# A fused attention and expert layer: the last expert's rows placed by a zero-one product, and the two partial sums of a tile added on Pool

## The reference

```python
x = layer_norm(DN_ALPHA * x + fox_mixer(x, ...), ln1_g[0], ln1_b[0])
y = moe(x, ...)
x = layer_norm(DN_ALPHA * x + y, ln2_g[0], ln2_b[0])

def moe(...):                 # the routed part
    # each token goes to 8 of 64 experts, with weights w
    def body(acc, blk):
        rows, rw, e = blk
        xb = x_pad[rows]
        h = jax.nn.silu(xb @ w_gate[e]) * (xb @ w_up[e])
        yb = (h @ w_down[e]) * rw[:, None]
        return acc.at[rows].add(yb), None
    shared = (jax.nn.silu(xf @ ws_gate) * (xf @ ws_up)) @ ws_down
    return acc[:T] + shared

def layer_norm(x, g, b):
    mu = jnp.mean(x, -1, keepdims=True)
    var = jnp.mean(jnp.square(x - mu), -1, keepdims=True)
    return (x - mu) * lax.rsqrt(var + LN_EPS) * g + b
```

## Time and profile before

| | |
|---|---|
| median of 3 runs | 1689.19 us (1687.73 to 1690.91) |
| profiled execution, its own time | 1685.87 us |
| its span, first to last instruction | 1684.2 us |
| busy share PE, DVE, ACT, POOL | 93%, 70%, 61%, 31% |
| mean granted clock of PE | 0.964 of full speed |

### The profile page before, as it was taken

How to read it: one execution, slowest core, us unless ns; L and a number is a source line. 1 busy time by engine, 2 the same in 40 slices (tenths; PEclk the granted TensorE clock), 3 DMA queues, 4 the chain that set the end, 5 groups by cost and what they waited for, 6 DMA issues and landing times.

```text
span 1684.2 us, 31748 instructions
## 1 busy us (share of the span) xinstructions
PE 1565.4 (93%) x8182; PEld 1306.1 (78%) x8183; DVE 1181.8 (70%) x2034; ACT 1027.7 (61%) x1700; POOL 514.2 (31%) x486
## 2 busy tenths in 40 slices
PE   6999999999998998998999999999999999999960
PEld 6897888888887776786878878888788878788840
DVE  3215777777778777746777867777677778778827
ACT  3215666666667544336667867667676777678823
POOL 0000000000000145423455445455455554465320
PEclk9999999999999998998999999999999999999975
DMA  7223221222224425569899999989998999999957
GB/s 239 88 79 98 65 70 46 69 57 62 69 50 138 177 107 177 190 212 345 238 304 312 324 360 334 306 251 285 314 318 256 306 362 314 359 355 351 365 125 294
DMA packets 161508, 369.25 MB, mean 219 GB/s; under 512 B 53040, under 2 KB 73520, under 8 KB 161456
## 3 DMA queue, kind: packets, MB, share of 16 engines
q1 hardware_dynamic: 136272, 284.21, 48.4%
q0 software_dynamic: 25184, 84.39, 19.7%
HBM read 294.39 MB, written 65.77 MB: 214 GB/s over the span
## 4 chain that ended last, share of the span: by engine, by line
PE 66%; DMA 11%; DVE 9%; issue 6%; ACT 3%; POOL 1%; POOLq 1%; ACTq 1%; another core or an unknown queue 0%; SPq 0%; DVEq 0%
DMA sums_scratch<-ys,sidx 7%; PE bank L993 5%; PE bank L996 5%; PE bank L999 5%; PE out_ps L884 4%; PE q_ps L88 4%; PE q_ps L90 4%; PE q_ps L89 4%; PE out_ps L1051 3%; PE k_ps L863 3%; PE out_ps L1052 3%; PE k_ps L1020 3%; PE q_ps L983 3%; PE k_ps L1021 3%; PE k_ps L1028 2%
## 5 line engine op out<-in xcount | busy, mean ns | idle before, releaser
L1836 DVE TENSOR_TENSOR gu_lo<-raw_gu,gu_hi 128x1024 fp32r<-128x1024 f32 x260 | 306.4, 1220 | 25.2 <-ACT gu_hi L1330 24.1
L1330 ACT CAST gu_hi<-raw_gu 128x1024 fp32r<-128x1024 f32 x260 | 253.3, 1050 | 2.3 <-DMA raw_gu<-in_moe_w_gate_dram 1.2
L993 PE MATMUL bank<-gu_hi,xb_hi 128*128 128x512 f32 x576 | 233.9, 406 | 6.2 <-DVE gu_lo L1836 3.1
L996 PE MATMUL bank<-gu_lo,xb_hi 128*128 128x512 f32 x576 | 227.9, 396 | 0.0
L664 POOL DMA_INDIRECT sums_scratch<-ys,sidx x64 | 122.6, 1916 | 155.3 <-DMA sums_scratch<-ys,sidx 112.5
L1836 DVE TENSOR_TENSOR dn_lo<-raw_dn,dn_hi 128x1024 fp32r<-128x1024 f32 x130 | 152.3, 1209 | 3.7 <-ACT dn_hi L1330 3.7
L999 PE MATMUL bank<-gu_hi,xb_lo 128*128 128x512 f32 x576 | 142.5, 389 | 0.0
L643 POOL DMA_INDIRECT x_rows<-rows_scratch,gidx x64 | 83.6, 1306 | 173.8 <-DVE wcol L1852 141.2
L993 PEld LDWEIGHTS bank<-gu_hi,xb_hi 128*128 128x128 f32 x576 | 110.6, 192 | 29.7 <-issue 7.5
L1330 ACT CAST dn_hi<-raw_dn 128x1024 fp32r<-128x1024 f32 x130 | 130.0, 1051 | 3.2 <-DMA raw_dn<-in_moe_w_down_dram 3.2
L599 POOL IOTA e<- 128x64 f32 x1 | 0.2, 190 | 427.6 <-DVE xs L1632 427.6
(11 more groups left out here) (276 smaller groups left out, 3934.6 us busy)
## 6 DMA issues: line engine op xcount, KB each, us to landing
raw_gu<-in_moe_w_gate_dram SPq DMA_DIRECT2D x128, 512.0 KB
raw_gu<-in_moe_w_up_dram SPq DMA_DIRECT2D x128, 512.0 KB
raw_dn<-in_moe_w_down_dram SPq DMA_DIRECT2D x128, 512.0 KB
wqk<-in_fox_w_in_dram SPq DMA_DIRECT2D x66, 128.0 KB, 2.5
v_scratch<-v_out SPq DMA_DIRECT2D x32, 256.0 KB, 2.8
va<-v_scratch SPq DMA_DIRECT2D x16, 512.0 KB, 4.7
xs<-in_x_dram SPq DMA_DIRECT2D x8, 512.0 KB, 7.8
wv<-in_fox_w_in_dram SPq DMA_DIRECT2D x4, 1024.0 KB, 6.1
```

What stands on the lines that cost most here:

```text
L993: i = pe.matmul(o3, xb_hi[s][:, c], g_hi[:, :, c], start=c == 0, stop=False, skip_group_check=True)
L996: pe.matmul(o3, xb_hi[s][:, c], g_lo[:, :, c], start=False, stop=False, skip_group_check=True)
L1330: a.copy(hi, raw).then_inc(S[done], 1)
L1836: dve.tensor_tensor(lo, raw, hi, ALU.subtract).then_inc(S[lo_ok], 1)
```

## The change

The first rows and the last further block of expert 63 are no longer added in memory.

- ACT and DVE write the scaled rows of expert 63 as a high and a low part, `y_hi` and `y_lo` (128 x 1024), and the last further block as `yx_hi`, `yx_lo` (64 partitions: its two stacked halves).
- POOL writes `tokens` (an iota of 0 to 1023 on every partition); DVE compares it with the token of each row and gets a zero-one matrix `place_of` (128 rows by 1024 tokens), and `x_place` for the further rows. The tokens of the rows come from `tab` (`tok_f`, `tok_x`).
- PE multiplies: for each tile of 128 tokens, `place_of` with `y_hi` and `y_lo`, `x_place` with `yx_hi` and `yx_lo`, 8 matmuls of 128 x 512 into `q_ps` or `k_ps` in turns (`put_in_place`). The result is what expert 63 adds to each token of the tile.
- On PE the first rows of expert 63 now go in front of the end of its further block: `turn_h` before `gate_up_further`, `down` before `turn_h_further`.
- POOL no longer issues the two adds of expert 63. It raises `summed` before `add_first` of 62, and after that adds the two sums of each tile (`fin0 <- fin0 + fin1`, 128 x 1024, eight of them, semaphore `f_pair`).
- SP loads `sums[1]` of tiles 0 and 1 on `summed`, then waits for `sent[0]` and `sent[1]`, which now end with expert 62, then loads the rest.
- DVE's sum of a tile takes PE's PSUM tile and POOL's sum. g2 is copied once by ACT into `out_ps`, and DVE reads it there; the output tile is written over `fin1` instead of a buffer of its own.

```diff
@@ SP
             sp.wait_ge(S["g_lo_ok"], G_PIECES * (E + 1))
-            sp.wait_ge(S["set_free"], 1)
             sp.wait_ge(S["summed"], 1)
-            load_sums(1, 0)
+            for t in range(2):
+                load_sums(1, t)
             for i in range(2):
-                sp.wait_ge(sent[i], 8 * E + SENT_0[i])
-            for t in range(TT):
+                sp.wait_ge(sent[i], 8 * E + SENT_0[i] - 16 * i)
+            for t in range(2):
                 load_sums(0, t)
-                if t + 1 < TT:
-                    load_sums(1, t + 1)
+            for t in range(2, TT):
+                load_sums(1, t)
+                load_sums(0, t)
@@ POOL, in expert(63), ahead of add_first of 62
+                if ends:
+                    pool.wait_ge(S["d_lo_ok"], D_PIECES * E)
+                    g.iota(tokens[:], pattern=[[1, T]], base=0, channel_multiplier=0, allow_small_or_imprecise_dtypes=True).then_inc(S["f_pair"], 1)
...
+                        pool.sem_inc(S["summed"], 1)
                     add_first(1 - par, e - 1)
@@ POOL, the end
-            with pool.If(nx > 0):
-                add_further(E - 1, nx - 1, xi + nx - 1)
-            add_first(1, E - 1)
-            pool.wait_ge(sent[2], 16 * (xi + nx) + SENT_0[2])
-            stand(pool)
-            pool.sem_inc(S["summed"], 1)
+            for t in range(TT):
+                pool.wait_ge(tile_in[t], 16 * 3)
+                g.tensor_tensor(fin0[:, t], fin0[:, t], fin1[:, t], ALU.add).then_inc(S["f_pair"], 1)
@@ PE
+            def put_in_place(further_too):
+                for t in range(TT):
+                    to = slice(t * P, (t + 1) * P)
+                    if t == 0:
+                        pe.wait_ge(S["place_step"], 2)
+                    if t >= 2:
+                        pe.wait_ge(S["f_mean"], 2 * (t - 2) + 1)
+                    for r in HALVES:
+                        o = (q_ps, k_ps)[t % 2][:, r]
...
+                        pe.matmul(o, place_of[:, to], y_hi[:, r], start=True, stop=False, skip_group_check=True)
...
+                        i = pe.matmul(o, place_of[:, to], y_lo[:, r], start=False, stop=not further_too, skip_group_check=True)
...
+                            pe.matmul(o, x_place[:, to], yx_hi[:, r], start=False, stop=False, skip_group_check=True)
+                            i = pe.matmul(o, x_place[:, to], yx_lo[:, r], start=False, stop=True, skip_group_check=True)
@@ ACT
+                        last_y_hi(m, e)
+                        act.wait_ge(S["x_downed"], after)
+                        a.copy(yx_hi[:, 0:D], out_ps[0:2 * XR, :]).then_inc(S["y_hi_ok"], 1)
...
+                    a.copy(out_ps[:], g2[:]).then_inc(S["y_hi_ok"], 1)
@@ DVE
+            dve.tensor_scalar(place_of[:, 0:T], tokens[:], tok_f[:, 0:1], None, ALU.is_equal).then_inc(S["place_step"], 1)
...
+                dve.tensor_scalar(x_place[:], tokens[0:2 * XR], tok_x[:, 0:1], None, ALU.is_equal).then_inc(S["place_step"], 1)
...
-                    dve.tensor_tensor_reduce(out=fin0[:, t], in0=fin0[:, t], in1=fin1(t), scale=1.0, scalar=0.0, op0=ALU.add,
+                    dve.tensor_tensor_reduce(out=fin0[:, t], in0=(q_ps, k_ps)[i][:], in1=fin0[:, t], scale=1.0, scalar=0.0, op0=ALU.add,
...
-                    dve.scalar_tensor_tensor(out=fin2[:, t], in0=fin0[:, t], scalar=fnm[i][:, 0:1], in1=g2[:], op0=ALU.add,
+                    dve.scalar_tensor_tensor(out=fin1[:, t], in0=fin0[:, t], scalar=fnm[i][:, 0:1], in1=out_ps[:], op0=ALU.add,
```

More of the change, by code:

```diff
@@ L254, in build @@
             tab = sb("tab", [P, TAB], I32, c=m)
+            tok_f = sb("tok_f", [P, 1], c=m)
+            tok_x = sb("tok_x", [2 * XR, 1], c=m)
         with ExitStack() as f:
             fin0 = sb("fin0", [P, TT, D], c=f)
-            fin2 = sb("fin2", [P, TT, D], c=f)
+            y_hi = sb("y_hi", [P, D], F32R, c=f)
+            y_lo = sb("y_lo", [P, D], F32R, c=f)
+            tokens = sb("tokens", [P, T], c=f)
+            x_place = sb("x_place", [2 * XR, T], F32R, c=f)
+            place_of = sb("place_of", [P, T + E], F32R, c=f)
+            yx_hi = sb("yx_hi", [2 * XR, D + E], F32R, c=f)
+            yx_lo = sb("yx_lo", [2 * XR, D + E], F32R, c=f)
             g2 = sb("g2", [P, D], c=f)
@@ L731, in expert @@
                 else:
+                    if ends:
+                        with pool.If(nx > 0):
+                            pool.wait_ge(sent[2], 16 * (xi + nx - 1) + SENT_0[2])
+                            stand(pool)
+                        with pool.If(nx < 1):
+                            pool.wait_ge(sent[2], 16 * xi + SENT_0[2])
+                            stand(pool)
+                        pool.sem_inc(S["summed"], 1)
                     add_first(1 - par, e - 1)
@@ L1142, in expert @@
                     down(m - 1, par, e + 1)
+                    if last:
+                        pe.wait_ge(S["x_rows_lo_ok"], xi + nx)
+                        turn_h(m)
                     gate_up_further(w, xi + nx - 1)
+                    if last:
+                        down(m, w, e + 2)
+                        turn_h_further(xi + nx - 1)
+                        down_further(w, e + 2, xi + nx - 1)
+                        put_in_place(True)
                 with pe.If(nx < 1):
                     down(m - 1, par, e + 1)
+                    if last:
+                        turn_h(m)
+                        down(m, w, e + 2)
+                        put_in_place(False)
                 return xi, nx
@@ L1151, in _ @@
             expert(E - 2, 0)
-            xi, nx = expert(E - 1, 1, last=True)
-            with pe.If(nx > 0):
-                turn_h_further(xi + nx - 1)
-                down_further(0, E + 1, xi + nx - 1)
-            turn_h(SH + E - 1)
-            down(SH + E - 1, 0, E + 1)
+            expert(E - 1, 1, last=True)
         @block.scalar
@@ L1438, in further_y_half, with last_y_hi @@
                 a.copy(ys[2][0:XR], out_ps[XR:2 * XR, :]).then_inc(S["x_y_half"], 1)
+            def last_y_hi(b, e):
+                act.wait_ge(S["downed"], b + 1)
+                act.wait_ge(S["w_ok"], e + 1)
+                a.activation(y_hi[:], k_ps[:], ACT.Copy, scale=wcol[:, e:e + 1]).then_inc(S["y_hi_ok"], 1)
             def load_counts(e):
```

95 lines of the change are left out of this document (64 added, 31 removed).

## The result

| | before | after |
|---|---|---|
| median, runs of one comparison | 1688.65 us (16 runs, 1682.58 to 1694.43) | 1678.92 us (16 runs, 1672.52 to 1688.96) |
| profiled execution, own time | 1685.87 us | 1677.4 us |
| its span | 1684.2 us | 1675.7 us |

What follows compares the result with a forecast made beforehand. DVE bounds the norm's eight tiles, which start behind expert 63's add in memory and the loads. First sum 15.7 us earlier, less 3.7 us of new waits, gives -12.0: span 1672.2, median 1677.2 us; range 1672.3 to 1683.0.

Steps and rivals of the forecast that it cites:

- The gain's mechanism: Before the second norm: loads start when expert 62's add lands, 1626.2 in place of 1644.56; DVE's first sum 15.7 us earlier.
- the stretch before 1600: Ahead of the changed tail: if this part of the profile moves, the forecast is wrong.
- Landing and loads: Ahead of POOL's first add: expert 62's add lands about 6.9 us after issue, 0.4 DMA delay, 4.2 first pair's load.
- The iota: On POOL ahead of expert 62's add: 0.9 us for 1024 columns, costing nothing because POOL idles 5.39 us there.
- The tile add: POOL's sum of two inputs per tile: 2.1 us, twice the one-input row, bounds 1.04 and 3.1.
- The placing: PE's first tile of expert 63, placed at 1630.2 to 1632.6, before POOL's 1633.1 by 0.5 to 2.9 us: costs nothing.
- no engine is as slow as DVE: In the norm's eight tiles: PE 1.8 to 3.4 us a tile, loads 2.6, POOL 2.1, all under DVE's 3.92.
- The new wait: In the norm: DVE's two-SBUF-input operation waits for POOL's adds three times, 3.7 us in all, bounds 0 and 6.3.
- DVE does not wait: Rival in the norm: POOL's adds never hold DVE, giving -15.7 and 1673.5 us; chance 0.18.
- not let in between two adds: Rival in the norm: DVE's first L2014 waits for all eight POOL adds, 1682.9 us; chance 0.19 together with placing late.
- placing late: Rival before the first sum: first tile placed at 1635 to 1637, 1679 to 1681 us; 0.19 together with DVE not let in.
- POOL the bound: Rival in the norm: slow POOL tile adds set the pace, no gain at 4.5 us each, 1694.8 at 5.2; chance 0.04.

Runs made afterwards that it cites:

- third profile: The changed kernel once more, nothing edited, beside three edited kernels in the last comparison: median 1675.25 us, ratio 0.9922 to the kernel before; profiled span 1670.3 us.

## Why the prediction was right, and where it was not

The prediction's sum and the first profile, from one anchor to the next, in us:

| stretch | predicted | measured | difference |
|---|---|---|---|
| to the issue of expert 61's add | 1611.79 | 1611.10 | -0.7 |
| from there to expert 62's add | 7.5 | 12.4 | +4.9 |
| from there to DVE's first sum | 13.9 | 12.5 | -1.4 |
| from there to the end of the span | 39.0 | 39.7 | +0.7 |
| span | 1672.2 | 1675.7 | +3.5 |

- **The gain's mechanism is right.** The loads start when expert 62's add has landed; nothing else held them. In the third profile of the changed kernel, where the gather was quick as in the profile of before, it is 60.4 us from expert 61's add to the end of the span (1670.3 - 1609.89), against 72.4 before (1684.2 - 1611.79): 12.0 less, the figure of the sum.
- **The step that failed**, inside a sum that came out, is one that it took for granted: that expert 62's add is issued at 1619.31 as before, 7.5 us behind 61's. It came 12.4 us behind. The prediction named "the stretch before 1600" as what must not move, and did not look at the stretch between 1600 and 1620, where an indirect gather and two broadcast loads start within about 2 us of each other (the earlier trace rows hold the adds only). The change edits neither; SP waits for PE's `gated` ahead of the loads, and POOL issues the gather by its own progress. Whether the change made the bad order more frequent is open: one execution of before was profiled, and it had the good order; of the eight profiled after it whose loads were not moved, six had the gather late, one of them less.
- **Landing and loads were over-estimated.** Add 62 to POOL's first add was 11.7 us in the sum and took 10.0. In the chain of the changed kernel's third profile the landing and the load are 6.03 and 3.79 us, where the earlier trace rows had 6.86 and 4.23; the early loads of `sums[1]` cost nothing that could be seen:

```profile
1618.14 6.03 DMA sums_scratch<-ys,sidx
1624.18 3.79 DMA fin<-sums_scratch
1628.05 2.39 POOL fin L764
1630.59 1.22 DVE fin L2083
```

- **The iota** took 1.58 us, not 0.9, and was hidden, as said (POOL idles 9.66 us behind it, 4.66 in the third profile).
- **The tile add** took 2.35 us (9.38 / 4), not 2.1, inside the bounds 1.04 to 3.1. The estimate from the Trainium skill (GPSIMD Engine Reference, 3.1 Elementwise — side-by-side cycle accounting), 2.25 us, is nearer than my doubling of the earlier trace rows. One add does take about twice as long as on DVE (2.35 against 1.23 us), as that page has it; but its advice against such adds on this engine (4.1 Engine selection) does not hold here as a whole: by the trace the adds cost 1.3 us at the start and 4.45 beside DVE, but moving them to DVE costs more, 43.5 against 39.7 us of norm.
- **The placing is hidden**, by 1.3 us, as predicted (0.5 to 2.9). Its first tile ended at 1634.33 (the step at 1634.10 takes 0.23), later than the forecast 1630.2 to 1632.6, but with everything else behind the gather. The clock was at the upper level (2.4 GHz) until then, 7 us longer than I said; from 1634.42 the steps are 0.43:

```profile
1623.00:1634.00 11.00, 9.02 (x39) 6.77 (x38) 5.63 (x10) 3.90 (x6) 2.45 (x2) 1.00 0.58 143
1634.00:1642.00 8.00, 8.00 (x19) 4.52 (x17) 5.44 (x11) 4.41 (x7) 8.00 (x4) 0.54 0.98 391
```

The columns are those of the earlier trace rows; the granted clock goes from 1.00 to 0.54. PE is busy all through the second stretch. At the lower level (1.2 GHz) the second tile's 8 steps take 3.85 us (1634.42 to 1638.27) and each later tile 4.0:

```profile
1638.27 0.79 PE L1100 MATMUL q_ps<-y_hi,place_of 128*128 128x512 f32 x1
...
1642.27 0.79 PE L1100 MATMUL k_ps<-y_hi,place_of 128*128 128x512 f32 x1
```

That is above DVE's period of 3.92. The prediction had 1.8 to 3.4 us for PE and said that no engine is as slow as DVE; on this point it was wrong. It costs nothing with eight tiles only because PE starts ahead: with b2 in PSUM the last matmul of the third tile starts 1.85 us before its sum on DVE (1637.27 and 1639.12), that of the eighth 1.38 (1657.30 and 1658.68).
- **The new wait** was there, three times, 4.45 us where I had 3.7: right in mechanism and count, 0.7 short. With an add of 2.35 in place of 2.1 the same working gives 0.5 + 2.1 + 2.1 = 4.7. What I said it would look like, idle time ahead of L2099, is wrong: it is in the duration.
- **Rivals.** "DVE does not wait" fell to the durations of L2099; "not let in between two adds" to L2099 ending 1.1 us behind the end of the add that was running when it came, each time; "placing late" only by 1.3 us, and becomes true with PE's order of before; "POOL the bound" would have needed 4.5 us an add.

That the first median lies 1.7 us from the forecast is luck in part: a late gather I had not priced (+4.9 in some executions) and landings shorter than priced (-1.4), and my offset of 3.3 us from profile to median, which was 1.5 here (1678.92 - 1677.4).

## What to carry to other kernels

Take an accumulation in memory off the tail by making its last term a product in PSUM: the chain of a landing and the loads behind it goes, and the extra engine work is hidden if it fits beside the previous landing. When a second engine then works on the same SBUF tiles, count for each operation of DVE how many inputs lie in SBUF, and put a constant that is read in every step into PSUM. And compare the period of every engine at the lower clock as well: PE's 4.0 us a tile here is more than DVE's 3.92 and, by an estimate from these two, would set the pace in a longer loop. List every transfer that is issued within a few us of one on the path, even if the edit touches neither: their order can flip from run to run, and moving a load away from one victim can put it in front of the next.

## What the runs showed of the hardware

- An indirect gather of 32 rows takes 3.4 to 4.2 us from issue to first use when the two 512 KB loads that spread a row over all partitions are issued 1.7 us or more behind it, 7.0 us when they come 0.34 us behind it, and 8.4 to 8.7 us when it is issued 0.1 to 0.4 us behind them. What in the queues does this was not tried.
- These two loads take 6.9 and 8.6 us from issue to landing in the first profile (the DMA issues, last column in us), with 1 MB between them that at 411 GB/s would be 2.6:

```profile
g<-in_ln_g_dram SPq DMA_DIRECT2D x1, 512.0 KB, 6.9
b<-in_ln_b_dram SPq DMA_DIRECT2D x1, 512.0 KB, 8.6
```

- A POOL add of two float32 128 x 1024 inputs takes 2.35 to 2.4 us; a DVE operation with two SBUF inputs that comes while it runs lasts until about 1.1 us behind the add's end, and counts as busy meanwhile. POOL's wait shows the same way: in the third profile the add that starts while such a DVE operation (1641.19 to 1644.23) is not yet done takes 3.10 us.

```profile
1643.36 3.10 POOL L764 TENSOR_TENSOR fin<-fin 128x1024 f32<-128x1024 f32 x1 [0.21 <-DMA fin<-sums_scratch]
```

- An iota of 1024 float32 columns on POOL takes 1.58 us, hardly less than one of 1856 int32 columns, 1.68, so the one could not be scaled by its columns to the other.
